# ScalarE beside the gather: a slot's coefficient ahead of its share of the mixer's part

## The chip, the cores and the metric

The kernel runs on one core of one Trainium2 chip. The metric is the device time of one execution in microseconds (us), taken as the median of three runs: 2354.31 us, with 2352.12 and 2357.56 at the ends. One further execution was recorded by the profiler; it took 2355.03 us, and its span, from the first to the last instruction, is 2353.2 us.

## The reference, cut to what matters

The reference is two transformer blocks one behind the other. The part that matters here is the second block, whose two layers each end in a retrieval layer, `peer_ffn`. For each of 256 tokens it picks 8 heads x 16 experts and mixes their rows:

```python
idx = jnp.take_along_axis(cand_i, pos, axis=-1)
g = jax.nn.softmax(top_s, axis=-1).astype(xc.dtype)
act = jax.nn.gelu(jnp.einsum('td,thkd->thk', xc, u[idx]), approximate=False)
return jnp.einsum('thk,thkd->td', g * act, v[idx])
```

The rows `u[idx]` and `v[idx]` (1024 numbers each) stand side by side in memory. Between the first layer's `peer_ffn` and the second's stands a mixer, here a differential attention:

```python
x = layer_norm(DEEPNORM_ALPHA * x + gate * f, ln_g[i, 0], ln_b[i, 0])
...
s = jnp.where(dist >= 0, s, -jnp.inf)
p = jax.nn.softmax(s, axis=-1)
a = p[:, :, 0] - lam_full * p[:, :, 1]
return jnp.einsum('bhqk,bkhe->bqhe', a.astype(v.dtype), v)
```

## The kernel before, in words

The 256 tokens are two tiles of 128. The two retrieval layers are cut into 512 **slots**: 2 layers x 2 tiles x 128 experts (8 heads x 16). A slot is one expert for each of 128 tokens, that is 128 gathered rows of 8 KB, 1 MB. It passes through four engines:

- POOL issues the gather of slot s (L520) into one of 8 buffers (`RING`), once TensorE has released that buffer from slot s - 8 (`slot_used`).
- VectorE, in `dot(s)` (L2344), waits for the landing and multiplies `u` with the token's row.
- ScalarE, in `coefficient(s)`, waits for the dot product; `gelu(s)` makes GELU (L1486), times the gate (L1490), times the identity matrix (L1491). At every sixteenth slot it also makes the exponentials of a head's gate (`gate_exp`, L1496). GELU, Exp and Sqrt each need another activation table, which `ACT_TABLE_LOAD` brings.
- TensorE, in `slot(s)` (L943), multiplies this diagonal with `v`, adding into PSUM, and releases the buffer.

The gathers of one tile run beside the dense work on the other. While slots 128 to 255 run, the mixer and the next layer's queries are made for tile 0 (`mixer_parts(0)`), while slots 256 to 383 run, for tile 1 (`mixer_parts(1)`), and while slots 384 to 511 run, the last norm of tile 0 (`last_parts(0)`). Each of these is a generator on TensorE, VectorE and ScalarE alike, with 56 parts for a mixer and 11 for the last; a `yield` ends a part. `parts_due(s)` and `parts_begun(s)` spread 56 parts over 92 slots, so that 0 or 1 part begins at a slot, and the same part number begins at the same slot on VectorE and ScalarE. TensorE runs a part 3 slots earlier (`PE_AHEAD`). VectorE runs its part ahead of `dot(s)`.

Within a mixer stand, in this order: a layer norm (`norm_parts`: the row copy L1503, the square L1517, the root L1520, the scaling L1524 on ScalarE), six weight products (row copies L1530, turned copies L1534), the attention in four **pairs** of heads, a norm over heads (the square L1582, the root L1585), two weight products, a second layer norm, and the four products of the queries. A pair goes: TensorE's scores (L1018); VectorE's masking and maximum (`masked`, L2264, L2267); ScalarE's exponentials (`exps`, L1561) in the part of the same number; VectorE's join of the two softmaxes in the next part (`joined`, L2273 to L2278), which waits for the exponentials; TensorE's transposes (L1026); ScalarE's copies (`turned`, L1569); TensorE's values (L1034).

Waits are on semaphores, and each engine takes its instructions in the order in which they are written. The order on ScalarE beside the gather is this loop:

```python
for s in range(early, N_SLOTS):
    for _ in range(parts_begun(s)):
        next(beside[s // SLOTS])
    coefficient(s)
```

Of the kernel before, what the change touches and what calls it, by code (L numbers as in the profile page):

```python
# [62 lines left out]
def parts_due(s):  # L63
    n = (0, PARTS_MIXER, PARTS_MIXER, PARTS_LAST)[s // SLOTS]
    return max(0, min(n, (s % SLOTS - 3) * n // 92 + 1))


def parts_begun(s):
    return parts_due(s) - (parts_due(s - 1) if s % SLOTS else 0)
# [62 lines left out]
def build(nc, xT_in, w_stream, wf_in, c_in, ada_w, tab_in, vec_in, alibi_in, subkeys, experts, lam_in, subln_in, out, out_rows):  # L132
    ctx = ExitStack()
    with ctx:
# [1055 lines left out]
        def _(act):  # L1190
# [292 lines left out]
            def gelu(s):  # L1483
                r = s % RING
                act.wait_ge(dot_done, s + 1)
                link(af(gel8[:, r:r + 1], act8[:, r:r + 1], ACT.Gelu))  # L1486
                if s % PK == 0:
                    act.wait_ge(gate_ready, s // PK + 1)
                at = s % SLOTS
                link(af(coef8[:, r:r + 1], gel8[:, r:r + 1], ACT.Copy, scale=gate[:, s // SLOTS % 2, at:at + 1]))  # L1490
                af(diag[:, r], ident, ACT.Copy, scale=coef8[:, r:r + 1]).then_inc(diag_ready, 1)  # L1491

            def gate_exp(n):

                act.wait_ge(ts_shift, n + 1)
                af(gexp[:, n % 2], ts_[:, n // PEER_HEADS % 2, n % PEER_HEADS], ACT.Exp, bias=gmax[:, n % 2:n % 2 + 1],  # L1496
                   accum_out=gsum[:, n % 2:n % 2 + 1]).then_inc(ts_exp, 1)
# [130 lines left out]
            def last_parts(t):  # L1628
                copy_f(t, 4 + t)
                yield  # L1630
                yield from norm_parts(4 + t)
                for n in range(4):
                    for b in range(2):
                        act.wait_ge(row_turned, TURNS_DENSE + 2 * n + b + 1)
                        af(tile_rows[:, n, b * TILE_N:(b + 1) * TILE_N], banks[4 + b][:, :], ACT.Copy,
                           scale=1.0 if n else ALPHA).then_inc(row_copied, 1)
                    yield
                yield

            def last_rows():  # L1640

                af(warm[:, :], vcol("eps", 0), ACT.Sqrt)
                act.wait_ge(mean2_done, 6)
                act.wait_ge(res2_done, 7)
                link(af(sq_row, r_row, ACT.Square, bias=end_nmean, accum_out=end_ss))
                af(end_rt, end_ss, ACT.Sqrt, scale=1.0 / D, bias=vcol("eps", 2)).then_inc(rt3_done, 1)
# [38 lines left out]
            def coefficient(s):  # L1685

                gelu(s)
                if s % PK == 2 and s < (TURNS - 1) * PK:
                    gate_exp(s // PK + 1)
                if s == LAM_AT:  # L1690
                    act.wait_ge(lam_sum, 1)
                    af(lexp, lsum, ACT.Exp).then_inc(lam_exp, 1)
# [27 lines left out]
            act.dma_start(skT, subkeys[1]).then_inc(sk_landed, 16)  # L1720
            beside = [None, mixer_parts(0), mixer_parts(1), last_parts(0)]
            for s in range(early, N_SLOTS):
                for _ in range(parts_begun(s)):
                    next(beside[s // SLOTS])
                coefficient(s)
            last_rows()


# [860 lines left out]
```

## Time and profile before

| what | value |
|---|---|
| median of three runs | 2354.31 us (2352.12 to 2357.56) |
| profiled execution, its span | 2355.03 us, 2353.2 us |
| busy share of the span: PE, DVE, ACT, POOL | 88%, 68%, 47%, 28% |
| `dot` L2344: count, mean | 512, 1243 ns |
| coefficient on ScalarE: L1486, L1490, L1491, means | 201, 295, 401 ns |
| `slot` L943 on PE: matmuls, mean | 2048 (4 a slot), 623 ns |
| gathers L520: count, median from issue to landing | 512, 14.5 us |
| gathered bytes (queue q0) | 587.24 MB |
| ACT's table loads from 1000 us on, each | 1283 ns |

The span falls into a first part with the first block and the second block's first mixer (to about 940 us), and the 512 slots behind it, to 2340 us, which the last rows' norm ends. The second part is read from the line of GB/s in 40 slices, and from stretches of it.

### The profile page before, as it was taken

To read this page: it belongs to the slowest core of one execution; us is meant where nothing else is said; L and a number is where in the kernel's file an instruction comes from. 1 tells how busy PE (TensorE), PEld (TensorE's weight loads), DVE (VectorE), ACT (ScalarE), POOL (GpSimd) and SP (SyncE) were. 2 spreads that over 40 slices of the span, in tenths; PEclk is the share of its full clock that TensorE was granted. 3 is DMA by queue.
4 is the path that set the end of the run, shared out by engine and by line. 5 is a ranking of instruction groups with operands and counts; after the bars stand their busy time and mean duration, and the time that the engine had idled before them with its cause. 6 is when DMAs were issued, how large, how long until landed. Compare 5 with 4: busy or idle time off the path is not lost.

```text
span 2353.2 us, 28200 instructions
## 1 busy us (share of the span) xinstructions
PE 2082.0 (88%) x9734; PEld 1329.5 (56%) x9734; DVE 1594.2 (68%) x3700; ACT 1112.4 (47%) x2730; POOL 652.2 (28%) x624
## 2 busy tenths in 40 slices
PE   7789998998999989888778988987999998888876
PEld 6769998777999987433223444432444443333322
DVE  5836678755778869767667476556658656676654
ACT  5445534444643445444445365444547444454543
POOL 0000010100001007544433243343334334434342
PEclk9899999999999998999999999999999999999999
DMA  6215596832679647999999999999999999999997
GB/s 233 90 36 181 177 330 227 293 126 81 209 248 353 220 157 288 382 420 419 421 420 417 418 418 420 389 420 419 415 421 402 401 382 420 420 420 421 420 420 305
DMA packets 131349, 768.22 MB, mean 326 GB/s; under 512 B 14481, under 2 KB 16273, under 8 KB 59281
## 3 DMA queue, kind: packets, MB, share of 16 engines
q0 software_dynamic: 87552, 587.24, 61.4%
q1 hardware_dynamic: 42944, 177.81, 21.1%
q8 instruction: 71, 1.16, 0.2%
q10 hardware_dynamic: 720, 1.51, 0.2%
q14 instruction: 62, 0.50, 0.1%
HBM read 765.45 MB, written 1.05 MB: 326 GB/s over the span
## 4 chain that ended last, share of the span: by engine, by line
PE 51%; DMA 27%; DVE 12%; ACT 6%; issue 3%; POOL 1%; SPq 0%; ACTq 0%; DVEq 0%; POOLq 0%
DMA arena<-experts,arena 26%; PE bank L943 13%; PE bank L554 9%; PE bank L556 8%; PE bank L555 8%; PE bank L977 6%; DVE arena L2344 4%; PE bank L691 1%; ACT arena L1491 1%; ACT arena L1279 1%; ACT arena L1490 1%; POOL arena L520 1%; PE bank L656 1%; DVE wlo L1750 1%; DVE arena L1860 1%
## 5 line engine op out<-in xcount | busy, mean ns | idle before, releaser
L943 PE MATMUL bank<-arena 128*128 128x512 f32 x2048 | 992.5, 623 | 168.3 <-ACT arena L1491 168.1
L2344 DVE CUSTOM_DVE_ANT_0 arena<-arena 128x1024 f32<-128x1024 f32 x512 | 635.7, 1243 | 465.4 <-DMA arena<-experts,arena 464.6
L520 POOL DMA_INDIRECT arena<-experts,arena x512 | 567.8, 1109 | 835.5 <-PE bank L943 794.3
L943 PEld LDWEIGHTS bank<-arena 128*128 128x128 f32 x2048 | 376.7, 195 | 736.8 <-ACT arena L1491 377.0
L1205 ACT CAST whi<-wring 128x1024 fp32r<-128x1024 f32 x228 | 238.3, 1049 | 255.6 <-PE bank L556 247.9
L1486 ACT ACTIVATE arena<-arena 128x1 f32<-128x1 f32 x512 | 103.0, 201 | 507.3 <-DVE arena L2344 505.8
L1750 DVE TENSOR_TENSOR wlo<-wring,whi 128x1024 fp32r<-128x1024 f32 x216 | 263.3, 1224 | 116.3 <-ACT whi L1205 115.6
L1491 ACT ACTIVATE arena<-tab,arena 128x128 f32<-128x128 f32 x512 | 205.5, 401 | 16.7
L506 POOL DMA_DIRECT2D arena<-ada_w x64 | 34.0, 532 | 646.9 <-DVE adaM L1797 628.4
L554 PE MATMUL bank<-hTh,whi 128*128 128x256 f32 (+2 forms) x584 | 173.2, 297 | 17.4 <-DVE hTl L1759 9.3
L556 PE MATMUL bank<-hTh,wlo 128*128 128x256 f32 (+2 forms) x584 | 167.8, 287 | 0.0
L555 PE MATMUL bank<-hTl,whi 128*128 128x256 f32 (+2 forms) x584 | 167.8, 287 | 0.0
L1490 ACT ACTIVATE arena<-arena 128x1 f32<-128x1 f32 x512 | 150.8, 295 | 16.6
L977 PE MATMUL bank<-wring,hfT 128*128 128x512 f32 x320 | 145.8, 599 | 4.4 <-DVE hfT L2245 4.4
L554 PE MATMUL bank<-mTh,whi 128*128 128x272 f32 (+1 forms) x512 | 146.2, 286 | 0.0
L555 PE MATMUL bank<-h1l,whi 128*128 128x272 f32 (+1 forms) x512 | 145.8, 285 | 0.0
L555 PE MATMUL bank<-mTl,whi 128*128 128x272 f32 (+1 forms) x512 | 145.8, 285 | 0.0
L554 PE MATMUL bank<-h1h,whi 128*128 128x272 f32 (+1 forms) x512 | 145.6, 284 | 0.0
L556 PE MATMUL bank<-h1h,wlo 128*128 128x272 f32 (+1 forms) x512 | 145.4, 284 | 0.0
L556 PE MATMUL bank<-mTh,wlo 128*128 128x272 f32 (+1 forms) x512 | 145.4, 284 | 0.0
L554 PEld LDWEIGHTS bank<-hTh,whi 128*128 128x128 f32 (+1 forms) x584 | 112.1, 192 | 24.5 <-issue 18.6
L555 PEld LDWEIGHTS bank<-hTl,whi 128*128 128x128 f32 (+1 forms) x584 | 112.4, 192 | 1.2 <-issue 0.9
(330 smaller groups left out, 2991.7 us busy)
## 6 DMA issues: line engine op xcount, KB each, us to landing
wring<-w_stream SPq DMA_DIRECT2D x236, 512.0 KB, 3.7
wring<-w_stream SPq DMA_DIRECT2D x48, 1024.0 KB, 9.1
arena<-ada_w POOLq DMA_DIRECT2D x64, 512.0 KB, 5.4
alibi<-ada_w POOLq DMA_DIRECT2D x32, 512.0 KB, 5.4
arena<-experts,arena POOLq DMA_INDIRECT x512, 14.5
xT<-xT_in SPq DMA_DIRECT2D x1, 1088.0 KB, 5.1
alibi<-alibi_in ACTq DMA_DIRECT2D x1, 1024.0 KB, 4.9
tab<-tab_in SPq DMA_DIRECT2D x1, 831.0 KB, 6.8
```

The costliest lines, as they stand in the source:

```text
L520: pool.indirect_dma_start(g_ring[:, r], None, experts[n // (2 * PEER_HEADS)], bass.IndirectOffsetOnAxis(idx[:, s // SLOTS % 2, s % SLOTS:s ...
L554: mm(dst, a[0], b[0], start=start, stop=False)
L555: mm(dst, a[0], b[1], start=False, stop=False)
L556: return mm(dst, a[1], b[0], start=False, stop=stop)
L943: last = mm(banks[2 * t + b][:, :], diag[:, r], g_ring[:, r, D + b * TILE_N:D + (b + 1) * TILE_N], start=s % SLOTS == 0, stop=s % SLOTS == ...
L977: last = mm(dst, lhs[:, 4 * half + k], w[:, k * TILE_N:(k + 1) * TILE_N], start=half == 0 and k == 0, stop=half == 1 and k == 3)
L1205: nc.scalar.copy(whi[:, c], wring[:, g % 2, c]).then_inc(hi_done, 1)
L1486: link(af(gel8[:, r:r + 1], act8[:, r:r + 1], ACT.Gelu))
L1490: link(af(coef8[:, r:r + 1], gel8[:, r:r + 1], ACT.Copy, scale=gate[:, s // SLOTS % 2, at:at + 1]))
L1491: af(diag[:, r], ident, ACT.Copy, scale=coef8[:, r:r + 1]).then_inc(diag_ready, 1)
L1750: v.tensor_tensor(wlo[:, g % 2, c], wring[:, g % 2, c], whi[:, c].bitcast(F32), ALU.subtract).then_inc(lo_done, 1)
L2344: v.tensor_tensor_reduce(g_ring[:, r, 0:D], g_ring[:, r, 0:D], hrow[:, t], 1.0, 0.0, ALU.mult, ALU.add, act8[:, r:r + 1]).then_inc(dot_don ...
```

## The change

ScalarE's loop beside the gather calls `coefficient(s)` first and then the part that begins at this slot. Nothing else is changed; the other engines' instructions stand as before.

```diff
             beside = [None, mixer_parts(0), mixer_parts(1), last_parts(0)]
             for s in range(early, N_SLOTS):
+                coefficient(s)
                 for _ in range(parts_begun(s)):
                     next(beside[s // SLOTS])
-                coefficient(s)
             last_rows()
```

The order on ScalarE at two places shows it. The gate's exponentials (L1496) belong to the coefficient of their slot and so keep their place, and the shift is seen against them. The first place is the second pair of heads of tile 1, from the gate's exponentials behind slot 290's coefficient to the pair's exponentials (L1561). L1486, L1490 and L1491 are one coefficient. Before:

```order
L1496 ACT_TABLE_LOAD
L1496 ACTIVATE arena<-arena 128x16
L1486 ACT_TABLE_LOAD
L1486 ACTIVATE arena<-arena 128x1
L1490 ACTIVATE arena<-arena 128x1
L1491 ACTIVATE arena<-tab,arena 128x128
L1561 ACT_TABLE_LOAD
L1561 ACTIVATE arena<-arena 128x256 x4
```

Now, over the same stretch:

```order
L1496 ACT_TABLE_LOAD
L1496 ACTIVATE arena<-arena 128x16
L1486 ACT_TABLE_LOAD
L1486 ACTIVATE arena<-arena 128x1
L1490 ACTIVATE arena<-arena 128x1
L1491 ACTIVATE arena<-tab,arena 128x128
L1486 ACTIVATE arena<-arena 128x1
L1490 ACTIVATE arena<-arena 128x1
L1491 ACTIVATE arena<-tab,arena 128x128
L1561 ACT_TABLE_LOAD
L1561 ACTIVATE arena<-arena 128x256 x4
```

The pair's exponentials moved behind one more coefficient, that of slot 292, whose dot product VectorE makes after this pair's masking. The other three pairs of tile 1 and the four of tile 0 moved in the same way. The number of table loads on ScalarE is 108 in both. The second place is the second layer norm of tile 0, again behind gate exponentials, those of slot 194. Before, the square L1517 stands behind one coefficient:

```order
L1496 ACT_TABLE_LOAD
L1496 ACTIVATE arena<-arena 128x16
L1486 ACT_TABLE_LOAD
L1486 ACTIVATE arena<-arena 128x1
L1490 ACTIVATE arena<-arena 128x1
L1491 ACTIVATE arena<-tab,arena 128x128
L1517 ACTIVATE sqt<-xnt 128x1024
L1486 ACTIVATE arena<-arena 128x1
```

Now it stands behind two:

```order
L1496 ACT_TABLE_LOAD
L1496 ACTIVATE arena<-arena 128x16
L1486 ACT_TABLE_LOAD
L1486 ACTIVATE arena<-arena 128x1
L1490 ACTIVATE arena<-arena 128x1
L1491 ACTIVATE arena<-tab,arena 128x128
L1486 ACTIVATE arena<-arena 128x1
L1490 ACTIVATE arena<-arena 128x1
L1491 ACTIVATE arena<-tab,arena 128x128
L1517 ACTIVATE sqt<-xnt 128x1024
```

The square moved behind the coefficient of its own slot, 196, and so behind that slot's dot product on VectorE and its landing.

## Rows read from the trace of the kernel before

**Rows 1.** The page: GB/s moved, in 40 slices of the span.

```profile
GB/s 233 90 36 181 177 330 227 293 126 81 209 248 353 220 157 288 382 420 419 421 420 417 418 418 420 389 420 419 415 421 402 401 382 420 420 420 421 420 420 305
```

**Rows 2.** Busy time by stretch; the last columns: PE clock, DMA share, GB/s.

```profile
1240.00:1640.00 400.00, 359.21 (x944) 161.71 (x944) 255.27 (x688) 193.76 (x543) 153.52 (x135) 0.97 1.00 414
1640.00:2025.00 385.00, 351.09 (x951) 160.72 (x952) 252.52 (x676) 191.52 (x528) 149.13 (x130) 0.98 1.00 408
...
1475.00:1500.00 25.00, 25.00 (x74) 12.18 (x74) 15.89 (x39) 12.99 (x39) 13.38 (x10) 1.00 0.93 364
...
1775.00:1800.00 25.00, 23.75 (x89) 12.56 (x88) 23.75 (x74) 20.19 (x59) 12.48 (x11) 1.00 0.97 381
```

**Rows 3.** Waits, 1000 to 2350 us: in total, times, longest.

```profile
POOL arena L520 <- PE bank L943: 776.5, 423, 9.6
...
DVE arena L2344 <- DMA arena<-experts,arena: 447.6, 382, 3.7
...
ACT arena L1530 <- PE bank L977: 100.9, 16, 8.1
```

**Rows 4.** Timeline of DVE, tile 1: each pair's dot product and the join behind it.

```profile
1753.57 1.28 DVE L2344 CUSTOM_DVE_ANT_0 arena<-arena 128x1024 f32<-128x1024 f32 x1
...
1757.17 0.15 DVE L2273 RECIPROCAL arena<-arena 128x2 f32<-128x2 f32 x1
...
1762.82 1.22 DVE L2344 CUSTOM_DVE_ANT_0 arena<-arena 128x1024 f32<-128x1024 f32 x1
...
1766.24 0.15 DVE L2273 RECIPROCAL arena<-arena 128x2 f32<-128x2 f32 x1
...
1774.45 1.23 DVE L2344 CUSTOM_DVE_ANT_0 arena<-arena 128x1024 f32<-128x1024 f32 x1
...
1776.20 0.16 DVE L2273 RECIPROCAL arena<-arena 128x2 f32<-128x2 f32 x1
...
1783.53 1.23 DVE L2344 CUSTOM_DVE_ANT_0 arena<-arena 128x1024 f32<-128x1024 f32 x1
...
1785.82 0.16 DVE L2273 RECIPROCAL arena<-arena 128x2 f32<-128x2 f32 x1
```

**Rows 5.** Timeline of DVE, tile 0: the same of its fourth pair.

```profile
1394.74 1.23 DVE L2344 CUSTOM_DVE_ANT_0 arena<-arena 128x1024 f32<-128x1024 f32 x1
...
1397.03 0.16 DVE L2273 RECIPROCAL arena<-arena 128x2 f32<-128x2 f32 x1
```

**Rows 6.** Timeline of ACT, tile 1, fourth pair: coefficient, then the exponentials.

```profile
1781.31 0.20 ACT L1486 ACTIVATE arena<-arena 128x1 f32<-128x1 f32 x1 [0.78 <-DVE arena L2344]
...
1782.29 1.28 ACT L1561 ACT_TABLE_LOAD   x1
1783.58 0.51 ACT L1561 ACTIVATE arena<-arena 128x256 f32<-128x256 f32 x1
...
1784.59 0.49 ACT L1561 ACTIVATE arena<-arena 128x256 f32<-128x256 f32 x1
```

**Rows 7.** Timeline of PE, tile 1: slots 291 and 292.

```profile
1761.96 1.98 PE L943 MATMUL bank<-arena 128*128 128x512 f32 x4
1767.62 3.60 PE L943 MATMUL bank<-arena 128*128 128x512 f32 x4 [3.68 <-ACT arena L1491]
```

**Rows 8.** Timeline of POOL, tile 1: the gathers of slots 299, 300 and 308.

```profile
1764.22 0.94 POOL L520 DMA_INDIRECT arena<-experts,arena  x1 [1.55 <-PE bank L943]
1771.49 0.94 POOL L520 DMA_INDIRECT arena<-experts,arena  x1 [6.34 <-PE bank L943]
...
1791.97 1.88 POOL L520 DMA_INDIRECT arena<-experts,arena  x1 [0.78 <-PE bank L943]
```

**Rows 9.** Timeline of DVE, then ACT, then PE: second norm of tile 0.

```profile
1466.28 1.22 DVE L2344 CUSTOM_DVE_ANT_0 arena<-arena 128x1024 f32<-128x1024 f32 x1
...
1467.22 1.04 ACT L1517 ACTIVATE sqt<-xnt 128x1024 f32<-128x1024 f32 x1
...
1468.31 3.78 PE L967 MATMUL bank<-sqt,tab 128*128 128x128 f32 x16 [4.29 <-ACT sqt L1517]
```

## The prediction, made before the changed kernel was run

> **What bounds the kernel now.** I read the line of GB/s first [rows 1]. The first 17 slices move anything between 36 and 382; from slice 18 on (about 1000 us) nearly all stand at 415 to 422. The change touches only this second part, and there the queues of transfers are full: the end comes when the last of the gathered bytes has come, so time is lost only where the rate falls. In the line that is slice 26 (389) and slices 31 to 33 (401, 402, 382). By stretches [rows 2] the rate is 414 over 400 us of tile 0's mixer and 408 over 385 us of tile 1's. Against 420 this is 400 x 6/420 = 5.7 us and 385 x 12/420 = 11.0 us of transfer time lost, 16.7 us in all; in the 25 us stretches at 1475 and at 1775 it is 25 x 56/420 = 3.3 and 25 x 39/420 = 2.3 us. The rest of the 512 slots has nothing to lose or win.
>
> Next the waits [rows 3]. POOL waits 776.5 us for TensorE to release a buffer: so a gather leaves when slot s - 8 is through VectorE, ScalarE and TensorE. VectorE waits 447.6 us in 382 of the slots for a landing, which says that mostly the chain behind the landing is quick enough. It isn't in two kinds of places, and both are in the mixers: where TensorE stands still for ScalarE's share of a part, and where VectorE runs without a gap. In the stretch from 1775 us VectorE is busy 23.75 of 25 us [rows 2], and the rate has fallen. I read that stretch by engine, from the timelines.
>
> **The change part by part.** Nothing is added or taken away; 108 table loads stand in both. ScalarE's part comes one coefficient later, and this coefficient waits for VectorE's dot product of the same slot. For VectorE and TensorE, what waits for ScalarE's part comes later; what waits for the coefficient comes earlier.
>
> *The pairs, tile 1.* VectorE masks, then makes the dot product of that slot, and joins in the next part. Before, ScalarE's exponentials ran beside that dot product. Now they follow it. Behind the start of the dot product it takes 1.23 us for the product [rows 4], 0.98 us for the coefficient (from 1781.31 to the table load at 1782.29), 1.28 us for the table load, and about 1.1 us until the first head's two exponentials are in (1783.58 to 1784.59, and a little for the semaphore) [rows 6]: 4.6 us. The join began 3.6, 3.4, 1.75 and 2.3 us behind the start of the dot product in the four pairs (1753.57 to 1757.17, 1762.82 to 1766.24, 1774.45 to 1776.20, 1783.53 to 1785.82) [rows 4]. So VectorE now stands still for 1.0, 1.2, 2.9 and 2.3 us, 7.4 us in all, queued behind it the next dot products. It has no idle time there to take this up.
>
> On the other side, slot 292's coefficient no longer stands behind the exponentials. TensorE waited 3.68 us for it and then ran slot 292 in 3.60 us where slot 291 took 1.98 [rows 7]; so the release comes up to 4 us earlier, and gather 300, which left 7.3 us behind gather 299 [rows 8], closes a hole. I count 0.9 us for this. Of the 7.4 us everything else reaches the gathers, since the queue has no reserve there (the rate is already down): +6.5 us. Bounds: -2.3 us (the whole loss of that stretch is won back by earlier coefficients) and +7.4 us.
>
> *The pairs, tile 0.* The same, with exponentials half as wide, so about 4.4 us in place of 4.6: the fourth pair's join comes at 2.3 us (1394.74 to 1397.03) [rows 5], 2.1 us too soon, and the other three, by the same subtraction in the same timeline, 0.4, 1.0 and 2.7 us: 6.2 us. Here the rate does not dip, so there is a reserve. A gather's landing takes 14.5 us at the median and its 1 MB 2.5 us at 420 GB/s; with four gathers under way in place of six the reserve is some 4 us. I take +2.0 us; bounds 0 and +6.2 us.
>
> *The norms.* In the second norm of tile 0 the square began at 1467.22, and TensorE waited 4.29 us for it [rows 9]. Now it is behind the coefficient of the slot whose dot product ends at 1466.28 + 1.22 = 1467.50: 1467.54 + 0.98 = 1468.5, 1.3 us later. The root that follows waits for TensorE's sums and moves with it; its own table load and coefficient lie beside those sums (3.78 us). TensorE's slots and so the gathers move by as much, in a stretch that already loses 3.3 us: +1.3 us. Tile 1's second norm is the same with 1.0. The first norm of each mixer begins with a row copy that now has a table load and a coefficient ahead of it, 1.28 + 0.98 = 2.3 us, but the queue is full there; 0.5 us each, bounds 0 and 2.3. The norm over heads: its root now waits for a dot product and a coefficient more, 2.2 us, and TensorE's next weight product for it; hidden by the same reserve in tile 0; 0.5 us for both, bounds 0 and 4.4. Row copies and turned copies of the weight products: ScalarE waits for TensorE there (100.9 us for L977 at L1530 [rows 3]), its dot products are long made, so the coefficient goes into this wait: nothing, in either direction.
>
> *Outside the mixers* the rate is 420 and stays so: a part comes every eighth slot, and a delay of 2.3 us is less than one gather.
>
> Weighed against the trace: a table load takes 1.28 us and the next activation starts 0.01 us behind its end (1782.29, 1783.58) [rows 6]. The Trainium skill (ScalarE: Activation LUTs, What ACT_TABLE_LOAD costs) puts a drain of about 1.38 us on top of each switch. By that rule each pair would wait 1.4 us more, and the pairs would cost up to 11 us more in all. The trace shows no such drain, and the sum goes by the row.
>
> Sum: 6.5 + 2.0 + 1.3 + 1.0 + 1.0 + 0.5 = 12.3 us; less 0.8 us, as some of what is late at a pair or norm is late behind a dip that was there anyway: 11.5 us. From the profiled execution, 2355.03 us, this gives 2366.5; it stood 0.7 us over the median, so against the median 2354.31 it is 2365.8 us.
>
> **The rivals.**
> *Hidden.* The queue's reserve takes up the pairs too, as gathers stay 4 to 6 deep, and only the two second norms show: 1.3 + 1.0 = 2.3 us, 2356.6 us. For it: the rate is at 420 for tile 0's pairs. Against it: it is at 381 in tile 1's, with VectorE full.
> *Faster.* Coefficients come earlier, and where TensorE's wait for them is what holds the release, the dips shrink: 3.68 us at slot 292 [rows 7], more such in tile 0. If the stretches at 1475 and 1775 both got their whole rate back, it would be -3.3 - 2.3 = -5.6 us, 2348.7 us. It decides from the point at which VectorE's join is not held up longer than TensorE is relieved, that is under some 1 us a pair; the rows give 1.0 to 2.9. The Trainium skill (Perfetto Trace Analysis, Optimization Strategies) would have it so: where the matmul engine idles for another, relieve what it waits for.
> *In full.* No reserve helps, and the new waits of TensorE make its next slots slow, as slot 292 was (1.6 us, some four times): 7.4 + 6.2 + 2.3 + 4.6 + 4.4 + 6.4 = 31 us, 2385.6 us. For it: each stage feeds the next, ring of 8. Against it: TensorE has idle time in the pairs.
>
> **How the numbers follow.** The forecast has 0.60 (its own range 2360 to 2373), hidden 0.22, faster 0.08, in full 0.10. A measurement of this kernel can tell about 0.2%, 4.7 us, from no change. Faster by more than that: most of the faster case, 0.07. Within: the hidden case, 0.22, and the rest of the faster one, 0.01: 0.23. Slower: 0.70. The range of 8 in 10 reaches into the hidden case and half way to the full one: 2354 to 2376 us.
>
> **What would show it.** In the changed profile: VectorE's wait at L2273 for ScalarE's L1561, absent before, of 1 to 3 us in eight pairs, some 13 us in all; the square L1517 of tile 0's second norm 1 to 1.5 us later against its L2235, and TensorE's wait for it grown from 4.29 to about 5.5 us; the rate of the stretch of tile 1's mixer down from 408 to about 400, of tile 0's from 414 to about 410, and 420 elsewhere; TensorE's wait at slot 292 gone or under 1.5 us. The prediction is wrong if VectorE's wait is there and the rates of both stretches don't fall (hidden), if they rise (faster), or if there is no such wait, which would mean that the exponentials do not follow the dot product as I read it.

## The result and the profile after

The changed kernel takes 2372.26 us in the median of four runs (2369.96 to 2377.02), the kernel before 2354.29; the ratio is 1.0077 (95% interval 1.0055 to 1.0099), that is +18 us. Forecast was +11.5 us, that is 2365.8, with a range of 2354 to 2376. The profiled execution took 2372.69 us, its span is 2370.9 us.

The page of the changed kernel, GB/s in 40 slices, beside [rows 1]:

```profile
GB/s 232 90 30 184 176 328 230 294 117 81 219 256 342 222 148 316 392 419 419 421 420 406 422 379 406 404 420 420 403 421 345 394 380 418 420 420 421 420 420 306
```

The plateau has more and deeper dips (379 in slice 24, 345 in slice 31). Stretches of the changed kernel, columns as in [rows 2]; tile 1's mixer now ends later, so its stretch is 400 us long:

```profile
1240.00:1640.00 400.00, 353.95 (x934) 159.70 (x934) 250.34 (x675) 192.16 (x535) 143.72 (x133) 0.97 1.00 408
1640.00:2040.00 400.00, 355.98 (x957) 162.92 (x956) 255.26 (x685) 193.65 (x533) 147.82 (x132) 0.97 0.98 396
2040.00:2345.00 305.00, 246.87 (x580) 95.44 (x579) 199.32 (x469) 140.93 (x413) 128.91 (x121) 0.99 1.01 420
...
1780.00:1810.00 30.00, 22.95 (x78) 11.84 (x77) 24.03 (x79) 20.81 (x60) 9.43 (x8) 0.89 0.83 311
```

Against 420 GB/s tile 0's mixer loses 400 x 12/420 = 11.4 us and tile 1's 400 x 24/420 = 22.9 us, 34.3 us in place of 16.7: +17.6 us. That is the whole result, to within the rounding of the rates (half a GB/s over 400 us is 0.5 us). Outside the mixers the rate is 420, as before. The 30 us at 1780, where tile 1's third and fourth pair stand, run at 311.

The waits of the changed kernel (in total, times, longest), beside [rows 3]:

```profile
POOL arena L520 <- PE bank L943: 801.0, 427, 9.4
...
ACT arena L1530 <- PE bank L977: 56.9, 15, 5.9
...
DVE arena L2273 <- ACT arena L1561: 14.8, 8, 2.8
```

The last row is new: VectorE's join waits for the exponentials, eight times. (ScalarE's wait ahead of the row copies, L1530, fell from 100.9 us, as its coefficient is now made inside that wait.) VectorE's timeline of the changed kernel shows the new waits one by one in tile 1, beside [rows 4]:

```profile
1760.93 1.28 DVE L2344 CUSTOM_DVE_ANT_0 arena<-arena 128x1024 f32<-128x1024 f32 x1
...
1765.66 0.17 DVE L2273 RECIPROCAL arena<-arena 128x2 f32<-128x2 f32 x1 [1.05 <-ACT arena L1561]
...
1776.16 0.17 DVE L2273 RECIPROCAL arena<-arena 128x2 f32<-128x2 f32 x1 [1.35 <-ACT arena L1561]
...
1784.56 1.22 DVE L2344 CUSTOM_DVE_ANT_0 arena<-arena 128x1024 f32<-128x1024 f32 x1
...
1789.23 0.17 DVE L2273 RECIPROCAL arena<-arena 128x2 f32<-128x2 f32 x1 [2.83 <-ACT arena L1561]
...
1801.38 0.17 DVE L2273 RECIPROCAL arena<-arena 128x2 f32<-128x2 f32 x1 [2.29 <-ACT arena L1561]
```

and in tile 0, the last of them beside [rows 5]:

```profile
1372.42 0.17 DVE L2273 RECIPROCAL arena<-arena 128x2 f32<-128x2 f32 x1 [0.83 <-ACT arena L1561]
...
1382.50 0.17 DVE L2273 RECIPROCAL arena<-arena 128x2 f32<-128x2 f32 x1 [1.81 <-ACT arena L1561]
...
1394.24 0.17 DVE L2273 RECIPROCAL arena<-arena 128x2 f32<-128x2 f32 x1 [2.62 <-ACT arena L1561]
...
1405.41 0.17 DVE L2273 RECIPROCAL arena<-arena 128x2 f32<-128x2 f32 x1 [2.00 <-ACT arena L1561]
```

From the start of the dot product to the join it is now 4.7 us in the first and third pair (1760.93 to 1765.66, 1784.56 to 1789.23). POOL's timeline shows where it arrives, beside [rows 8]; these are the gathers of slots 299, 300 and 308:

```profile
1775.18 0.94 POOL L520 DMA_INDIRECT arena<-experts,arena  x1 [3.05 <-PE bank L943]
1776.90 0.94 POOL L520 DMA_INDIRECT arena<-experts,arena  x1 [0.78 <-PE bank L943]
...
1808.57 0.94 POOL L520 DMA_INDIRECT arena<-experts,arena  x1 [5.14 <-PE bank L943]
```

Gather 300 follows gather 299 after 1.7 us in place of 7.3: the hole that slot 292 had left is closed. Part of it only moved, since TensorE now stops at slots 290, 291 and 293 instead (1.84, 1.57 and 1.75 us). Measured from slot 120, TensorE's release of a buffer is 7.0 us later than before at slot 288, 5.1 at slot 292 and 6.9 again at slot 296. And gather 308 leaves 31.7 us behind gather 300, where it was 20.5.

### The profile page after: what moved, and what is told of

The parts are those of the page before. It is cut to its first block, busy times and chain, and to the rows that moved or that the text cites. A ratio compares the mean times of both kernels' runs of the same rounds, so it can differ in the third digit from the quotient of the medians.

```text
span 2370.9 us, 28200 instructions
## 1 busy us (share of the span) xinstructions
PE 2082.4 (88%) x9734; PEld 1331.3 (56%) x9734; DVE 1595.3 (67%) x3700; ACT 1113.3 (47%) x2730; POOL 644.7 (27%) x624
## 3 DMA queue, kind: packets, MB, share of 16 engines
HBM read 765.45 MB, written 1.05 MB: 323 GB/s over the span
## 4 chain that ended last, share of the span: by engine, by line
PE 51%; DMA 24%; DVE 12%; ACT 8%; issue 3%; POOL 1%; SPq 0%; ACTq 0%; DVEq 0%; POOLq 0%
DMA arena<-experts,arena 23%; PE bank L943 13%; PE bank L554 9%; PE bank L556 8%; PE bank L555 8%; PE bank L977 7%; DVE arena L2344 4%; PE bank L691 1%; ACT arena L1491 1%; ACT arena L1490 1%; ACT arena L1279 1%; POOL arena L520 1%; ACT L1486 1%; DMA alibi<-ada_w 1%; PE bank L656 1%
## 5 line engine op out<-in xcount | busy, mean ns | idle before, releaser
L520 POOL DMA_INDIRECT arena<-experts,arena x512 | 560.7, 1095 | 858.4 <-PE bank L943 819.2
L1486 ACT ACTIVATE arena<-arena 128x1 f32<-128x1 f32 x512 | 103.3, 202 | 588.3 <-DVE arena L2344 586.9
L1491 ACT ACTIVATE arena<-tab,arena 128x128 f32<-128x128 f32 x512 | 205.5, 401 | 16.7
L1490 ACT ACTIVATE arena<-arena 128x1 f32<-128x1 f32 x512 | 150.8, 295 | 16.6
L977 PE MATMUL bank<-wring,hfT 128*128 128x512 f32 x320 | 144.1, 593 | 2.9 <-DVE hfT L2245 2.9
```

What stands on the lines that cost most here:

```text
L520: pool.indirect_dma_start(g_ring[:, r], None, experts[n // (2 * PEER_HEADS)], bass.IndirectOffsetOnAxis(idx[:, s // SLOTS % 2, s % SLOTS:s ...
L977: last = mm(dst, lhs[:, 4 * half + k], w[:, k * TILE_N:(k + 1) * TILE_N], start=half == 0 and k == 0, stop=half == 1 and k == 3)
```

## The experiments

All are the kernel before with one edit, unless said otherwise; ratios are to the kernel before, measured beside them, with 95% intervals. The first four have ScalarE's loop in this form, with the condition of each (n counts a mixer's parts from 0):

```diff
+                n = parts_due(s) - 1
+                mixer = SLOTS <= s < 3 * SLOTS
+                ahead = parts_begun(s) and ({condition} if mixer else False)
+                if ahead:
+                    coefficient(s)
                 for _ in range(parts_begun(s)):
                     next(beside[s // SLOTS])
-                coefficient(s)
+                if not ahead:
+                    coefficient(s)
```

**Only the pairs.**

```diff
+                ahead = parts_begun(s) and (18 <= n < 29 if mixer else False)
```

> The coefficient goes first only at the 11 parts of the attention's pairs (parts 18 to 28 of each mixer); everywhere else the part goes first, as before. Joins theory (VectorE's join waits for exponentials that now follow the dot product): VectorE waits about 14 us at L2273 for L1561 in eight pairs, and this is the larger part of the +18 us: +9 to +13 us over before, ratio about 1.005, with the gathers of tile 1 late by 8 to 10 us behind slot 304. Rival, spread theory (every moved part costs a little, copies and norms as much as pairs): 22 of 123 moved parts, +3 us. Rival, relief theory (a later norm gives back what the pairs lose, as TensorE's wait for the square L1517 shrinks): the shift of TensorE's slots falls again between slots 192 and 200 and between 320 and 330, by 2 to 3 us each.

Measured: 1.0043 (1.0027 to 1.0058), +10.1 us. The wait is all there; the loop is six lines longer, so VectorE's L2273 is L2279 in this kernel's waits:

```profile
DVE arena L2279 <- ACT arena L1561: 14.5, 8, 2.8
```

The joins theory holds, the spread theory (+3 us) falls. On the relief theory: TensorE's release of slot 312's buffer, measured from slot 120's, is 10.9 us later than before, that of slot 324 9.2 us, and the last of all 8.8 us. So 1.7 us come back over the second norm of tile 1. That the norm absorbs lateness is not shown by this: the run below that moves only the copies, in which those slots are not late, also falls by 1.7 us over the same slots (from -1.1 to -2.8).

**All but the pairs.**

```diff
+                ahead = parts_begun(s) and (not 18 <= n < 29 if mixer else True)
```

> The complement of the first: the coefficient goes first everywhere but at the pairs' parts. Joins theory: no wait of VectorE at L2273; what is left is the row copy of each first norm (+1 us), the norm over heads and the second norms: +4 to +6 us over before. If costs add up, this and the first run sum to +18 us; if the norm over heads costs only where the pairs have emptied the queue first, the sum stays well under 18 (some 13 us). Spread theory: +15 us.

Measured: 1.0035 (1.0023 to 1.0047), +8.2 us, more than the +4 to +6 expected (the interval is 5.4 to 11.1). With the first run it makes 0.78%, the whole change 0.77%: the two halves add. So what the pairs do not explain costs by itself, and is nearly as large as they are.

**Only the norm over heads.**

```diff
+                ahead = parts_begun(s) and (29 <= n < 33 if mixer else False)
```

> The coefficient goes first only at parts 29 to 32 of each mixer, the norm over heads (copies L1580, square L1582, root L1585, copies L1590). In the changed kernel TensorE's slots slip by 1.8 us there in tile 0 and by 4.0 us in tile 1. By the theory that each chain costs by itself: TensorE reaches its transposes L950 some 2.5 us later in both tiles, and the time is +2 to +4 us. By the theory that it needs a queue emptied by the pairs: under +1 us, within what can be measured.

Measured: 1.0020 (1.0009 to 1.0031), +4.7 us. It costs by itself, without pairs that have emptied the queue. This run moves three steps of ScalarE: the square (part 29), the root (part 30) and, in part 32, the copies L1590 of the turned rows.

**Only the layer norms.**

```diff
+                ahead = parts_begun(s) and (n < 6 or 37 <= n < 43 if mixer else False)
```

> The coefficient goes first only at the parts of the two layer norms of each mixer (parts 0 to 5 and 37 to 42). By my prediction's terms: +1.3 and +1.0 us for the second norms, whose square L1517 TensorE waits for, and 0.5 us for each first one: +3.3 us. Where the second norm's loss is set by TensorE alone and not by the square, +1 us. If the coefficients made earlier help there, 0 or less.

Measured: 1.0015 (1.0004 to 1.0026), +3.5 us. The sum fits the prediction's +3.3. This and the run before make 0.35%, the same as all but the pairs; so the row copies and turned copies of the products cost nothing that can be measured, which here means to within some 4 us.

The other runs keep the line numbers of before.

**Within the pairs: only the exponentials.**

```diff
+                for step in ((lambda: coefficient(s), share) if SLOTS <= s < 3 * SLOTS and n in (18, 20, 22, 24) else (share, lambda: coefficient(s))):
+                    step()
```

> The coefficient goes first only at the four parts of each mixer in which ScalarE makes a pair's exponentials (L1561). Joins theory: this alone makes VectorE wait at L2273, some 14 us in eight pairs, and brings nearly all of the +8.8 us by which the last release of a buffer moved with the pairs' parts moved: +7.5 to +9 us. Rival, copies theory (the copies L1569, for which TensorE's values wait, carry half): VectorE's wait is there, but the time is +4 to +5 us.

Measured: 1.0046 (1.0031 to 1.0061), +10.8 us: as much as all the parts of the pairs.

**Within the pairs: only the copies of the transposes.** The condition is `n in (21, 23, 25, 27)`.

> The coefficient goes first only at the four parts of each mixer in which ScalarE copies a pair's transposes (L1569). Joins theory: no wait of VectorE at L2273, TensorE has work queued ahead of the values, so within 1 us of before. Copies theory: +4 us. Relief theory (a coefficient earlier by 0.6 us there fills a dip): -1 us.

Measured: 0.9997 (0.9987 to 1.0007). Nothing; the copies theory falls, and no relief can be measured.

**The wait made shorter, in the changed kernel.** VectorE's dot product goes ahead of the join:

```diff
-                for _ in range(parts_begun(s)):
-                    next(beside[s // SLOTS])
-                dot(s)
+                join = SLOTS <= s < 3 * SLOTS and parts_due(s) - 1 in (19, 21, 23, 25)
+                for step in ([lambda: dot(s)] if join else []) + [lambda: next(beside[s // SLOTS])] * parts_begun(s) + ([] if join else [lambda: dot(s)]):
+                    step()
```

> The changed kernel, and on VectorE the four parts of each mixer that join a pair's softmaxes come behind the dot product of their slot, which gives the exponentials one dot product (1.23 us) more. Joins theory: VectorE's wait for L1561 falls from 14.8 us by 1.2 us for each join that waits as long, to about 5 us, and the time from +18 us to +12 to +14 us over before. Rival: VectorE's wait is only the sign, and ScalarE's coefficients stuck behind the later exponentials hold TensorE (it stands still 4.6 and 2.5 us at slots 297 and 300): then the wait falls and the time stays at +16 us or more.

Measured: 1.0052 (1.0038 to 1.0065), +12.2 us in place of +18. The wait fell by 7.8 us, less than expected, the time by some 6 us:

```profile
DVE arena L2273 <- ACT arena L1561: 7.0, 6, 1.7
```

TensorE's stop at slot 297, behind VectorE's longest wait, fell from 4.60 to 2.19 us. Its stop at slot 300 stayed, 2.47 us for 2.45: there the dot product had been ready for 4.6 us, and the coefficient stood behind a pair's exponentials and the table loads on both sides of them. So the rival's path exists beside that of the joins.

**The same, with only the exponentials' parts moved.** ScalarE's loop as in the run with the exponentials alone (the condition `n in (18, 20, 22, 24)`), and VectorE's edit above.

> The coefficient goes first only at the exponentials' parts, as in the run with these alone (+8 us, VectorE waits 14.4 us), and VectorE's joins come behind the dot product of their slot. Joins theory: the wait falls to about 5 us and the loss with it, to +2.5 to +4 us. Rival, coefficients stuck behind the exponentials: +6 us or more.

Measured: 1.0023 (1.0014 to 1.0032), +5.4 us in place of +10.8. The waits of the run with the exponentials alone, and of this one:

```profile
DVE arena L2273 <- ACT arena L1561: 14.4, 8, 2.8
```

```profile
DVE arena L2273 <- ACT arena L1561: 7.4, 6, 1.7
```

Half the wait, half the loss, and in both runs 0.23 to 0.25% less time. The absolute value lies between the two theories' bounds (+4 and +6) and its interval, 3.3 to 7.5 us, holds both, so it decides nothing by itself. What speaks for the joins is that the loss follows the wait in both runs, with ScalarE's order as it was. One rival stays open: the edit also makes a dot product, and with it its coefficient, ahead of the join's work on VectorE, and no run has this edit in the order of before.

**The two steps of the norm over heads, each alone.** The conditions are `n == 29` (copies and square) and `n == 30` (root).

> The coefficient goes first only at part 29 of each mixer: copies L1580 and square L1582 of the norm over heads. Two-step theory: the norm over heads costs two chained delays, one for the square (VectorE waits for it at L2291, some 2.5 us) and one for the root; this is the first, half of the run with both: +1.5 to +2.5 us. Single-step theory: the square's delay is hidden behind the root's table load, under 0.5 us.

> The coefficient goes first only at part 30 of each mixer: the root L1585 of the norm over heads. Two-step theory: VectorE's wait at L2294 grows from 1.2 by about 2.3 us in each tile, TensorE's transposes L950 come as much later: +1.5 to +2.5 us, the other half. Single-step theory: the whole +4 us stands here.

Measured: 0.9999 (0.9989 to 1.0009) for the square, 1.0000 (0.9990 to 1.0010) for the root. Each alone costs nothing that can be measured, up to 0.10%; the run above costs 0.20%, but it moves the copies L1590 as well, and neither square and root together nor the copies alone were run. TensorE's timelines in tile 0, at the transposes L950 that wait for this norm, first the run with all three steps (its L2302 is L2296):

```profile
1420.99 1.99 PE L943 MATMUL bank<-arena 128*128 128x512 f32 x4 [0.40 <-ACT arena L1491]
1427.89 1.97 PE L950 MATMUL bank<-tab,sqt 128*128 128x128 f32 x8 [4.92 <-DVE sqt L2302]
1429.66 5.46 PE L943 MATMUL bank<-arena 128*128 128x512 f32 x8
1435.11 3.70 PE L977 MATMUL bank<-wring,oT 128*128 128x512 f32 x8
```

the square alone:

```profile
1424.53 1.09 PE L950 MATMUL bank<-tab,sqt 128*128 128x128 f32 x8 [2.52 <-DVE sqt L2296]
1425.46 3.60 PE L943 MATMUL bank<-arena 128*128 128x512 f32 x8
1429.17 3.70 PE L977 MATMUL bank<-wring,oT 128*128 128x512 f32 x8
```

and the root alone:

```profile
1425.27 1.09 PE L950 MATMUL bank<-tab,sqt 128*128 128x128 f32 x8 [1.12 <-DVE sqt L2296]
1426.20 3.60 PE L943 MATMUL bank<-arena 128*128 128x512 f32 x8
1429.91 3.70 PE L977 MATMUL bank<-wring,oT 128*128 128x512 f32 x8
```

The delays stand in one chain. The square alone makes VectorE wait 1.28 and 0.87 us for it (tile 0, tile 1), and its wait for the root, 1.13 and 1.18 us before, is then gone, as in tile 0 the root starts 2.2 us behind the square's end in place of 4.4. So that delay is hidden, as the single-step theory had it; its other half, the whole loss in the root, did not come. The root alone lengthens that wait to 2.31 us in both tiles. With all three moved VectorE has both waits, 1.30 and 2.30 us in tile 0. The third step follows: TensorE's weight product L977 needs the copies L1590, and starts 7.2 us behind the transposes L950 in place of 4.6 (1427.89 to 1435.11, against 1424.53 to 1429.17). In tile 0 slow matmuls fill that time, in tile 1 a wait shows:

```profile
1815.81 1.97 PE L950 MATMUL bank<-tab,sqt 128*128 128x128 f32 x8 [3.96 <-DVE sqt L2302]
1817.57 4.36 PE L943 MATMUL bank<-arena 128*128 128x512 f32 x8
1823.03 3.70 PE L977 MATMUL bank<-wring,oT 128*128 128x512 f32 x8 [1.10 <-ACT oT L1590]
```

The clock is the other thing that differs. Stretches of the run with all three, and of the square alone (columns as in [rows 2]):

```profile
1425.00:1430.00 5.00, 2.11 (x9) 2.10 (x10) 4.82 (x8) 2.27 (x5) 0.00 (x0) 0.66 1.02 423
1430.00:1435.00 5.00, 5.00 (x8) 1.73 (x6) 4.89 (x14) 2.69 (x9) 0.97 (x1) 0.66 0.86 357
```

```profile
1425.00:1430.00 5.00, 4.89 (x16) 2.28 (x15) 4.89 (x15) 2.90 (x9) 1.60 (x2) 1.00 1.01 421
1430.00:1435.00 5.00, 5.00 (x13) 2.23 (x12) 4.76 (x11) 2.55 (x9) 0.76 (x2) 1.00 1.01 421
```

By the granted clock TensorE ran part of these 10 us at 1.2 GHz (0.66 in the mean) where the other run has 2.4 GHz throughout, and the rate falls in the second half. But such a stretch is not enough for a loss: in tile 1 the run with the root alone has a stop of 2.87 us, then slow matmuls (eight in 5.29 us) at the same mean clock, with the rate at 421, and its time is that of before:

```profile
1810.25 1.10 PE L950 MATMUL bank<-tab,sqt 128*128 128x128 f32 x8 [2.87 <-DVE sqt L2296]
1811.18 5.29 PE L943 MATMUL bank<-arena 128*128 128x512 f32 x8
```

```profile
1810.00:1815.00 5.00, 4.75 (x13) 2.48 (x14) 4.90 (x14) 2.76 (x8) 0.00 (x0) 0.66 1.01 421
```

Nor was the third delay enough: the first of the two runs below has it too, 7.1 us from L950 to L977 in both tiles, and no more time. How the 4.7 us are split between the three delays and the slow clock stays open. The profile cannot place them either. The buffer releases of the run with all three are, measured from slot 120's, 3.7 us later than before at the end, but 2.9 us of this stand at slot 140 already, ahead of anything that was moved.

**Two attempts at a faster kernel**, both in the order of before, by the place of the gate's exponentials:

```diff
-                if s % PK == 2 and s < (TURNS - 1) * PK:
+                if s % PK == 6 and s < (TURNS - 1) * PK:
```

and the same with 3.

> The order of before (part first), with the gate's exponentials (L1496, with a table load ahead and one behind, 3.0 us together) moved from the third to the seventh slot of each sixteen, so that they no longer stand ahead of the second norm's square L1517. If the square's lateness is what the second norms lose (TensorE waits 4.3 and 3.3 us for it), TensorE's wait shrinks by some 1.5 us in each and the time is -1 to -3 us. Rival: TensorE has too much work in that stretch anyway; the rate dips all the same, no change (within 1 us).

> The order of before, with the gate's exponentials behind the fourth coefficient of each sixteen. Twice in each mixer this puts them directly beside a part that needs the same table; 104 table loads in place of 108, 5.1 us of ScalarE's time saved, 2.6 us of it at the second pair of each tile. If in the pairs the coefficients stuck behind ScalarE's table loads hold the gathers (TensorE waits 3.7 us at slot 292), the time is -1 to -2 us; if VectorE alone sets the pace there, no change. The square of the second norm gets 0.4 us later, +0.5 us at most.

Measured: 1.0003 (0.9995 to 1.0012) and 1.0001 (0.9991 to 1.0011). With the first, TensorE's waits for the square L1517 in the mixers fell from 4.29 us and 3.3 us to 3.5 us for the two together,

```profile
PE bank L967 <- ACT sqt L1517: 3.5, 2, 2.3
...
DVE arena L2218 <- ACT arena L1496: 17.4, 6, 6.5
```

and the time stood. That does not clear the square: the second row, which the kernel before does not have, shows that the same edit made VectorE wait for the gate's exponentials instead. With 3, four table loads fewer (104) bought nothing either. No run here beats the kernel before.

## Why the prediction was right, and where its sum was short

The sum was 12.3 us before its deduction of 0.8, and the runs give 10.1 + 4.7 + 3.5 = 18.3 us for the same terms. Two thirds of the 6 us between them are the norm over heads.

- **The bound.** Right: all of the +18 us stands in the rate of the two mixers' stretches, nothing outside.
- **The pairs.** Right in mechanism and nearly in size. In tile 1 the waits read off beforehand, 1.0, 1.2, 2.9 and 2.3 us, came as 1.05, 1.35, 2.83 and 2.29. In tile 0, 0.4, 1.0, 2.7 and 2.1 us came as 0.83, 1.81, 2.62 and 2.00. All eight are 14.8 us, against some 13. The second pair of tile 0 is the miss (0.8 us). The gate's exponentials and their two table loads had held up ScalarE's coefficient of the slot before, so it began the pair's coefficient 2.1 us behind the start of the dot product (1377.19 to 1379.33) in place of 1.3. The distance had been read from a fourth pair, where no gate's exponentials stand ahead. The pairs' time was put at 6.5 + 2.0 = 8.5 us and measured at 10.1 us (interval 6.4 to 13.7). The exponentials' parts alone do it. That it goes through VectorE's wait is what the two runs with the join behind the dot product speak for; a run with that edit alone is missing.
- **The reserve.** In tile 1 there was none, as said. In tile 0, 4 us of 6.2 were to be taken up; the profile with only the pairs moved has TensorE's releases 6.7 us late at slot 176 and 3.3 us at slot 184, still 2.6 us at slot 224. That fits the +2.0, as far as one execution can tell.
- **The norm over heads.** This is the term that was mis-sized: "hidden by the same reserve in tile 0; 0.5 us for both". It is +4.7 us. The step that failed is the overlap: I had priced one delay of 2.2 us and let the reserve hide it. There are three in a chain, the square's, the root's and that of the copies L1590, each behind its own slot's coefficient; the copies had no term of their own. The square's and the root's are hidden when each is moved alone; the three together are not. The upper bound of 4.4 us was about right, the choice within it was not. Which of the three brings the loss, and how much of it is TensorE's slow clock, stays open.
- **The layer norms.** +3.3 us forecast, +3.5 measured, but not all as described. The square came 3.3 us behind VectorE's L2235 in place of 2.1, as forecast (1 to 1.5 later). TensorE's wait for it did not grow from 4.29 to 5.5 us, it shrank to 2.68. With only the layer norms moved it did grow, to 5.46 us, as forecast:

```profile
1469.55 3.79 PE L967 MATMUL bank<-sqt,tab 128*128 128x128 f32 x16 [5.46 <-ACT sqt L1517]
```

```profile
1471.84 1.22 DVE L2235 TENSOR_TENSOR xnt<-xnt,bank 128x1024 f32<-128x1024 f32 x1 [1.15 <-PE bank L962]
...
1475.11 1.04 ACT L1517 ACTIVATE sqt<-xnt 128x1024 f32<-128x1024 f32 x1
...
1476.20 3.15 PE L967 MATMUL bank<-sqt,tab 128*128 128x128 f32 x16 [2.68 <-ACT sqt L1517]
```

  The first is TensorE's row with only the layer norms moved, the others are VectorE's, ScalarE's and TensorE's rows in the changed kernel, beside [rows 9]. The reading of the wait was right, and missed that other parts, moved as well, bring TensorE to this norm late itself: its releases are 9.2 us behind at slot 192, just ahead of the norm, and 6.3 us at slot 198.
- **The rest.** Row copies, turned copies and the last part: nothing, right. The 0.8 us taken off the sum for overlap is not seen, as the parts add (0.43 + 0.20 + 0.15 = 0.78%), but each part is known only to within 3 or 4 us, so the runs could not show it.
- **The rivals.** Hidden fell with the rates. Faster fell too: TensorE's wait at slot 292 went, as forecast, but the releases gained only 1.9 us by it, and had lost them again at slot 296; at the two pairs behind, TensorE stood still 4.60 and 2.45 us. By the Trainium skill (Perfetto Trace Analysis, Optimization Strategies) one relieves what the matmul engine idles for; here the wait at slot 292 was relieved and the engine's idle time moved on and grew: its stops ahead of slots 288 to 313 are 12.2 us in all in place of 5.0. In full, 31 us, was too much; the slow passes behind TensorE's stops that it counted are seen, at slots 297 and 300. TensorE's timeline of the changed kernel there:

```profile
1787.19 1.98 PE L943 MATMUL bank<-arena 128*128 128x512 f32 x4
1793.78 3.24 PE L943 MATMUL bank<-arena 128*128 128x512 f32 x4 [4.60 <-ACT arena L1491]
...
1804.66 3.64 PE L943 MATMUL bank<-arena 128*128 128x512 f32 x4 [2.45 <-ACT arena L1491]
```

  The four matmuls of a slot take 1.98 us ahead of the first stop, and 3.24 and 3.64 us behind the two.

## What to carry to other kernels

Where two engines take turns beside a stream, moving an engine's share behind its stream step costs whatever the share ran beside: here the exponentials had been made during VectorE's next dot product, and now follow it. Read such a change off the timeline as the distance from one instruction to the one that waits, before and after; six of the eight waits came out within 0.2 us, and the widest miss, 0.8 us, stood where ScalarE had other work in its queue, which the distance has to include. Then count how many such delays stand in one chain before taking them as hidden: here two of the three cost nothing measurable when moved one at a time, and all three together 4.7 us.

## What the runs showed of the hardware

A TensorE stop of 4.92 us was followed by slow matmuls (eight in 5.46 us against 3.60, at a mean granted clock of 0.66), one of 2.52 us was not (1.00 throughout). But one of 2.87 us was (eight in 5.29 us, 0.66), and in the changed kernel one of 2.45 us, 11 us behind one of 4.60 us (four in 3.64 us against 1.98, at 0.70 in the 5 us from 1805), so the length of a stop alone does not tell.

A single execution says little about a microsecond or two: 27 runs of the kernel before on one chip went from 2346.09 to 2358.13 us. The one execution that is profiled can stand 3 to 5.5 us off its kernel's median: 2349.86 against 2353.12 us in the run with only the copies moved, 2349.44 against 2354.91 in the second attempt at a faster kernel.
